# Two transformer blocks on one core: the first norm's sum of squares on VectorE, one statistics pass for two norms in a row, and the end of the delta rule reordered

## The reference, cut to what matters

```python
x = first_block(x, attn_norm, w_in, ..., final_norm)      # DEPTH = 2 layers, ends with a norm
return second_block(x, c_2, ctx_2, ...)                   # one layer, starts with a norm

def rmsnorm(x, g):                                        # first block, its last line included
    return x * rsqrt(mean(x * x) + EPS) * g
# second block
hl = modulate(rmsnorm_2(xl, g_pre_mix[i]), sh1l, sc1l)    # the "recurrent" norm
hc = modulate(rmsnorm_2(xc, g_pre_mix[i]), sh1c, sc1c)    # the same for 256 context positions
... = mixer_inputs(hl, w_in) ; mixer_inputs(hc, w_in)     # projections ab, qkv, u, z
ol = bidir_gdn(ql, kl, vl, bl, gl, s_f, s_b)              # gated delta rule, 64-position chunks, both ways
y_f = fourier_mix(u, w_f)
y_d = rmsnorm_2(o, g_gdn) * silu(z)
y = concat([y_f, y_d]) @ w_out
xl = xl + gt1l * rmsnorm_2(y, g_post_mix[i])
```

## Time and profile before

| | us |
|---|---|
| median of 3 runs | 3139.52 |
| the three runs | 3134.92 to 3141.40 |
| the profiled execution: its time | 3141.11 |
| the profiled execution: its span, first to last instruction | 3139.3 |

### The profile page before, as it was taken

One profiled execution on the slowest core, in us unless ns is written; L12 is line 12 of the kernel. 1 busy time (PEld: TensorE's weight loads), 2 busy tenths in 40 slices (PEclk: granted clock), 3 DMA queues, 4 the chain that ended last, 5 costly groups with the idle time before them and its releaser, 6 DMA issues.

```text
span 3139.3 us, 41302 instructions
## 1 busy us (share of the span) xinstructions
PE 2963.7 (94%) x16704; PEld 2338.8 (75%) x16704; DVE 1448.9 (46%) x2527; ACT 738.4 (24%) x1585; POOL 1625.7 (52%) x1134
## 2 busy tenths in 40 slices
PE   6999999999999999999999999999899987699998
PEld 5767777777777877677777777778778676578886
DVE  2654443354555027544433545552342377277721
ACT  3333332112111023333321111211122223211110
POOL 5434445556555663344455565556535254556664
PEclk9999999999999999999999999999899999899999
DMA  5433444545666544344444456665434000345554
GB/s 183 164 121 134 147 142 168 170 149 173 230 233 225 193 161 169 122 144 138 148 161 154 154 167 235 242 231 189 153 121 147 1 3 22 107 147 189 199 189 141
DMA packets 133565, 491.99 MB, mean 157 GB/s; under 512 B 14832, under 2 KB 14832, under 8 KB 132608
## 3 DMA queue, kind: packets, MB, share of 16 engines
q1 hardware_dynamic: 70736, 260.86, 25.4%
q0 software_dynamic: 61200, 222.85, 19.7%
q10 hardware_dynamic: 1440, 5.64, 0.5%
HBM read 487.17 MB, written 2.13 MB: 156 GB/s over the span
## 4 chain that ended last, share of the span: by engine, by line
PE 82%; DVE 7%; POOL 5%; issue 3%; DMA 2%; ACT 1%; POOLq 0%; DVEq 0%; ACTq 0%
PE dense L740 22%; PE dense L742 21%; PE dense L741 21%; POOL raw_lo L2476 2%; PE scores L944 2%; PE O L978 2%; PE turned L966 1%; POOL squares_sum L2494 1%; PE scores L740 1%; PE scores L741 1%; PE scores L742 1%; DMA weights_hi<-stream 1%; PE O L1012 1%; DVE row_sum L1959 1%; PE dense L1136 1%
## 5 line engine op out<-in xcount | busy, mean ns | idle before, releaser
L2476 POOL TENSOR_TENSOR raw_lo<-raw,weights_hi 128x1024 fp32r<-128x1024 f32 x425 | 1021.9, 2405 | 81.6 <-DMA raw<-stream 38.9
L740 PE MATMUL dense<-h_hi,weights_hi 128*128 128x512 f32 x2208 | 890.3, 403 | 14.8 <-DVE h_lo L1783 10.2
L742 PE MATMUL dense<-h_hi,raw_lo 128*128 128x512 f32 x2208 | 867.3, 393 | 0.0
L741 PE MATMUL dense<-h_lo,weights_hi 128*128 128x512 f32 x2208 | 867.0, 393 | 0.0
L2466 POOL DMA_DIRECT2D weights_hi<-stream x425 | 244.8, 576 | 1169.1 <-PE dense L742 1058.6
L740 PEld LDWEIGHTS dense<-h_hi,weights_hi 128*128 128x128 f32 x2208 | 418.8, 190 | 141.7 <-issue 55.4
L742 PEld LDWEIGHTS dense<-h_hi,raw_lo 128*128 128x128 f32 x2208 | 418.4, 189 | 90.8
L741 PEld LDWEIGHTS dense<-h_lo,weights_hi 128*128 128x128 f32 x2208 | 419.4, 190 | 80.8
L740 PE MATMUL dense<-hidden_hi,weights_hi 128*128 128x512 f32 x528 | 206.2, 390 | 0.0
L741 PE MATMUL dense<-hidden_lo,weights_hi 128*128 128x512 f32 x528 | 205.6, 389 | 0.0
L742 PE MATMUL dense<-hidden_hi,raw_lo 128*128 128x512 f32 x528 | 205.5, 389 | 0.0
(11 more groups left out here) (374 smaller groups left out, 4427.5 us busy)
## 6 DMA issues: line engine op xcount, KB each, us to landing
raw<-stream SPq DMA_DIRECT2D x473, 512.0 KB, 3.5
weights_hi<-stream POOLq DMA_DIRECT2D x425, 512.0 KB, 4.6
decays<-stream ACTq DMA_DIRECT2D x8, 512.0 KB, 4.5
gates<-f_scratch SPq DMA_DIRECT2D x2, 1536.0 KB, 9.6
x<-x_in SPq DMA_DIRECT2D x2, 1024.0 KB, 8.3
dft<-dft SPq DMA_DIRECT2D x4, 512.0 KB, 6.7
out<-x SPq DMA_DIRECT2D x4, 512.0 KB, 2.6
const<-consts ACTq DMA_DIRECT2D x1, 1024.0 KB, 10.8
```

Source lines behind the costliest of these rows:

```text
L740: nc.tensor.matmul(to, wh, xh, start=first, stop=False)
L741: nc.tensor.matmul(to, wh, xl, start=False, stop=False)
L742: return nc.tensor.matmul(to, wl, xh, start=False, stop=final)
L2476: nc.gpsimd.tensor_tensor(lo, src, hi, ALU.subtract).then_inc(weights_lo, 1)
```

## The change

It has three parts.

1. **Start.** `const` is loaded in two parts: first the 512 columns from `ident` on (256 KB), then `cos`, `sin` and `tri` with a semaphore of their own (`rope_landed`), for which DVE, POOL and PE wait at later places. ACT squares all eight chunks into eight slots of their own; DVE adds them in seven additions. `norm_stats((0,1))` has one source, so four matmuls in place of eight. PE no longer waits for `init_done` before it. POOL waits for the second half of `x` alone, issues three weight loads, subtracts item 0, and only then waits for `init_done` and makes the power; item 1 comes after it.
2. **Between the blocks.** Norm "f" is gone. During the `down` products of layer 1 ACT squares each chunk twice, as it is and scaled by `final_norm`, and POOL adds both. One `norm_stats("L")` has 16 matmuls, one power has 8 columns, `norm_rows` makes the rows of the product of both norms and then those of the final norm alone. `xT` itself is scaled later, in pairs of chunks during qkv 1 to 4 (`final_x`). PE's order is ab (context), statistics, half of qkv 0, rows, the rest of the context blocks. The loads of `dft` and `wf` move behind the raw load of qkv 2 and wait for the eight chunks of "L".
3. **End of the delta rule.** The Fourier half's high parts are made by ACT in group 0 and its low parts by POOL in group 1. In steps 8 to 11 POOL adds `oscan` into `o2` before DVE adds the `dense` part. `w_out`'s first three items are subtracted two after step 8 and one after step 9. The position blocks 1 and 2, complete after step 9, are squared, summed and scaled during steps 10 and 11; the power is taken in two halves of 8 columns; the blocks go in the order `T_ORDER`.

```diff
+T_ORDER = (1, 2, 0, 3)
 # SP
-                if item == (1, "down", FC - 2):
-                    sp.wait_ge(hidden_lo_ready, DEPTH * FC)
-                    sp.wait_ge(h_ready, 8 * (NORMS["X"] + 1))
+                if item == (TAIL, "qkv", 2):
+                    sp.wait_ge(h_ready, 8 * (NORMS["L"] + 1))
                     for i in range(4):
                         sp.dma_start(dft[i], dft_in[i]).then_inc(s_dft, 16)
                     sp.dma_start(wf, wf_in).then_inc(s_dft, 16)
 # PE
+                if name == (0, 1):
+                    pe.wait_ge(first_added, 1)
+                for last_one in range(1 if name == (0, 1) else 2):
...
+                if name == "L":
+                    pe.wait_ge(f_added, ACC_STEPS)
+                    pe.wait_ge(f_squared, KC)
+                    for src in (acc_f, square_f[:, 1, :]):
+                        for t in range(TB):
+                            last = nc.tensor.matmul(O[:, TB + t:TB + t + 1], src[:, t * P:(t + 1) * P], ones[:, 0:1], ...)
...
-            pe.wait_ge(s_init, INITS)
...
-            norm_stats("f")
-            norm_rows("f")
-            fill(len(EARLY) * KC)
+            fill(KC)
             norm_stats("L")
+            fill(KC // 2)
             norm_rows("L")
+            fill(KC + KC // 2)
             fill(3 * KC)
...
-            for t in range(TB):
-                pe.wait_ge(p_dve, P_MEANS + t + 1)
+            for n, t in enumerate(T_ORDER):
+                pe.wait_ge(p_scaled, n + 1)
+                pe.wait_ge(c_o1, 2 * latent_no(STEPS))
 # ACT
-            act.dma_start(const, const_in).then_inc(s_const, 16)
+            act.dma_start(const[:, at:CONST_N], const_in[:, at:CONST_N]).then_inc(s_const, 16)
+            act.dma_start(const[:, 0:at], const_in[:, 0:at]).then_inc(rope_landed, 16)
...
-            squares("f", x_chunk(DEPTH - 1, "down"), xT)
-            squares("L", lambda k: act.wait_ge(h_ready, 8 * NORMS["f"] + k + 1), xT)
+            squares("L", x_chunk(DEPTH - 1, "down"), xT)
...
+                    if g == 0 and lev < LEVELS - 1:
+                        act.wait_ge(qk_ready, 2)
+                        nc.scalar.activation(four_hi[:, lev - 1, :], yT[:, lev - 1, :], ACT.Copy).then_inc(four_rounded, 1)
...
             for s in range(STEPS - 4, STEPS):
                 output_state(s)
+                if s == STEPS - 2:
+                    output_squares(0, 2 * latent_no(s))
+            output_squares(2, 2 * latent_no(STEPS))
 # DVE
+            for k in range(1, KC):
+                dve.wait_ge(squared, k + 1)
+                ...
+                nc.vector.tensor_tensor(acc, first, first_squares[:, k, :], ALU.add).then_inc(done, 1)
...
-            norm_var("f")
-            for k in range(KC):
-                norm_scale("f", k, lambda k: sm("final_norm", k), xT, xT)
-            norm_var("L")
+            nc.vector.tensor_scalar(eps_var[:], O[:, TB:2 * TB], EPS / D_MODEL, EPS * EPS, ...)
+            nc.vector.tensor_scalar(n_var[:, TB:2 * TB], O[:, TB:2 * TB], 1.0 / D_MODEL, EPS, ...)
+            nc.vector.scalar_tensor_tensor(out=n_var[:, 0:TB], in0=O[:, 0:TB], scalar=1.0 / D_MODEL, in1=eps_var[:], ...)
             shifted("L", 0, 0, 0, hx, xT, SEQ, KC)
...
+                if c in (1, 2, 3, 4):
+                    final_x(2 * c - 2)
+                    final_x(2 * c - 1)
...
             for s in range(STEPS - 4, STEPS):
                 new_values(s)
+                if s == STEPS - 1:
+                    output_scale(0)
                 new_state(s)
+                if s == STEPS - 2:
+                    output_sums(0)
+            output_sums(2)
+            output_gate(0)
+            output_scale(2)
+            output_gate(2)
 # POOL
-            pool.wait_ge(s_init, INITS)
-            pool.wait_ge(s_const, 16)
-            for step in range(2):
-                issue(step)
-            for step in range(1, KC - 1):
-                add_square((0, 1), step)
+            pool.wait_ge(s_x[1], 16)
+            for step in range(3):
+                issue(step)
+            low(0)
+            pool.wait_ge(s_init, INITS)
             norm_pow((0, 1))
-            low(0)
             low(1)
-            issue(2)
...
-            norm_pow("f")
+            norm_pow("L")
             low(N_LAYER_WEIGHTS + 2)
-            for step in range(1, KC - 1):
-                add_square("L", step)
-            norm_pow("L")
...
+                    if g == 1 and lev < LEVELS - 1:
+                        four_low(lev - 1)
...
+            add_output(8, kd_ready, 2 * UNITS)
+            low(W_OUT)
+            low(W_OUT + 1)
+            add_output(9, weights_lo, W_OUT + 2)
+            low(W_OUT + 2)
+            add_output(10, weights_lo, W_OUT + 3)
+            output_pow(0)
+            add_output(11, p_pow, 1)
+            output_pow(1)
             issue(W_OUT + 3)
```

More of the change, by code:

```diff
@@ L880, in norm_rows @@
                 last.then_inc(rows_ready, 1)
+                if name == "L":
+                    for t in range(TB):
+                        last = nc.tensor.matmul(turned[:, 0, t * P:(t + 1) * P],
+                                                rstd[:, TB + t:TB + t + 1].broadcast_to((P, P)), ident,
+                                                start=True, stop=True)
+                    last.then_inc(both_var, 1)
             def open_misc(l, what):
@@ L1366, in square_of @@
                     act.wait_ge(square_added, number * ACC_STEPS + max(1, k - 2))
+                if name == "L":
+                    at = SMALL["final_norm"] + k
+                    nc.scalar.activation(square[k % 2], src[:, k, :], ACT.Square, scale=small[:, at:at + 1]).then_inc(squared, 1)
+                    if k >= 2:
+                        act.wait_ge(f_added, max(1, k - 2))
+                    nc.scalar.activation(square_f[:, k % 2, :], src[:, k, :], ACT.Square).then_inc(f_squared, 1)
+                    return
                 nc.scalar.activation(square[k % 2][:, 0:n], src[:, k, 0:n], ACT.Square).then_inc(squared, 1)
@@ L1557, in _ @@
                 if l == 0:
-                    squares((0, 1), lambda k: act.wait_ge(s_x[k // 4], 16), xT)
+                    for k in range(KC):
+                        act.wait_ge(s_x[k // 4], 16)
+                        nc.scalar.activation(first_squares[:, k, :], xT[:, k, :], ACT.Square).then_inc(squared, 1)
                 else:
@@ L2398, in _, with output_sums, output_scale @@
                 w_and_u(g)
+            def output_sums(first):
+                for n in (first, first + 1):
+                    dve.wait_ge(p_sq, n + 1)
+                    nc.vector.tensor_reduce(osum[:, n * GH:(n + 1) * GH], heads(SQ4[n]), AX_X, ALU.add).then_inc(p_sum, 1)
+                both = osum[:, first * GH:(first + 2) * GH]
+                dve.wait_ge(p_sum, first + 2)
+                nc.vector.tensor_scalar(both, both, 1.0 / GD, EPS, ALU.mult, ALU.add).then_inc(p_var, 1)
+            def output_scale(first):
+                dve.wait_ge(p_pow, first // 2 + 1)
+                for n in (first, first + 1):
+                    o = heads(o2[T_ORDER[n]])
+                    nc.vector.tensor_tensor(o, o, per_head(oscale[:, n * GH:(n + 1) * GH]), ALU.mult).then_inc(p_scaled, 1)
@@ L2399, in _, with output_gate @@
+            def output_gate(first):
+                for n in (first, first + 1):
+                    t = T_ORDER[n]
+                    dve.wait_ge(p_turned, n + 1)
+                    z = zT[:, :, t * P:(t + 1) * P]
+                    nc.vector.scalar_tensor_tensor(out=z, in0=heads((bankB + bankA)[n]), scalar=half_gdn[:, 0:1], in1=z,
+                                                   op0=ALU.mult, op1=ALU.mult).then_inc(p_gated, 1)
             for s in range(STEPS - 4, STEPS):
                 new_values(s)
+                if s == STEPS - 1:
+                    output_scale(0)
```

152 lines of the change are left out of this document (90 added, 62 removed).

## The result

The changed kernel takes 3117.0 us in the median of four runs (3115.4 to 3120.4), the kernel before beside it 3138.8 (3134.9 to 3141.4): ratio 0.9935, 95% interval 0.9923 to 0.9946. That is faster by 21.8 us. The forecast was 3114.0, a gain of 25.6, with the range 3105 to 3122. The profiled execution took 3116.6 with a span of 3114.8, 24.5 less than the profiled execution before.

The account below looks back on a forecast made before the run. PE is busy 94% of the span, so only its standstills can be won: start 7.5, between the blocks 11.5, delta rule's end 7.0, less 0.4, is 25.6. From 3141.1 that gives 3115.5, adjusted to the median 3114; range 3105 to 3122.

Parts of the forecast that it names:

- low(0) ahead of power is the bound: Start: item 0's subtraction, awaiting its weight load, holds the power, which ends at 20.6 instead of 28.1; gain 7.5 us.
- my two readings of the queues: Start: POOL's load lands at 18.3 if it waits for SP's loads, 16.5 if sharing evenly; 17.1 taken.
- stays as it is: Start: the 5.3 us from the power's end to the first dense matmul remain unchanged.
- the lower bound of 6.2: Start: smallest gain in the forecast's range, in us, if POOL's weight load lands at 18.3.
- Rival A: Start: POOL's descriptors wait for DVE's seven additions, load lands at 18.9, gain 5.7, time 3116; 3 in 10.
- POOL's six more additions lie in `down` products of 15 us each ... cost nothing: Between the blocks: POOL's added work is covered and costs nothing; 7.7 us if that cover were gone.
- A wait for weights in the `down` products: Sign in the profile after that would show the forecast wrong; no size given.
- The term for the Fourier constants: Between the blocks: the 2.5 MB of `dft` and `wf` delay POOL's weight loads; 0.5 us taken.
- Rival C: Delta rule, steps 8 to 11: POOL's additions enter the recurrence, 10.4 us lost, time 3124.5; 0.5 in 10.
- B: Between the blocks: transfers hold weight loads back, half speed lasts through ab and qkv 0; gain 5, 3121; 1.5 in 10.
- D: Long dense stretches after the delta rule: clock at 1.2 GHz for longer, kernel slower than before; 2 in 100.
- E: Parts don't do what they say, such as the start still waiting at 12 us; 3132 or more; 3 in 100.

Follow-up runs that it names:

- power_first: The changed kernel with POOL's first power ahead of item 0's subtraction instead of behind it: 3114.9 us, ratio 0.9919.
- norms_only: The kernel before with only the part between the blocks changed: 3130.6 us, ratio 0.9975.
- late_add: The changed kernel with POOL's two additions of the first chunk's squares moved behind the next weight item's load and subtraction: 3115.2 us, ratio 0.9927.
- raws_late: The changed kernel with SP's third and fourth weight load held until POOL's first weight load has landed: 3113.8 us, ratio 0.9916.
- dft_later: The changed kernel with the Fourier constants loaded one by one behind the raw loads of qkv 4 to 8: 3113.2 us, ratio 0.9916.
- combo_stall: The changed kernel with power before subtraction, SP's two loads held, Fourier constants later, context low parts earlier; stall in `down` left in: 3112.2 us, ratio 0.9919.
- late_ctx_early: The changed kernel with the first chunk's additions moved later and DVE's context low parts one chunk of `down` earlier: 3113.5 us, ratio 0.9918.
- late_spread: The changed kernel with the first chunk's additions moved later and two context blocks between the halves of the statistics: 3120.4 us, ratio 0.9937.

## Why the prediction was right, and where it was wrong

**Start: right, 7.2 for 7.5, with some luck.** `x` landed at 10.35 (10.0), the first weight load at 18.3 (17.1), the power ended at 21.8 (20.6), and the first dense matmul started at 26.2 (26). The step "low(0) ahead of power is the bound" is shown by power_first. The landing was 1.2 late because the load started 0.5 later and took 7.6 us, above the 7.0 I had put between my two readings of the queues. So the power came 6.3 us earlier, not 7.5. I had written that the stretch from the power's end to the first dense matmul "stays as it is"; it went from 5.3 to 4.4 us, because DVE's first low part no longer stood beside POOL's second subtraction. I hadn't foreseen that, and without it the start would have been worth 6.3, near the lower bound of 6.2. Rival A gave 18.9 for the landing, which is near, but by the wrong mechanism. POOL issued its three loads in 1.81 us, 0.60 each, while DVE added; elsewhere an issue takes 0.58:

```profile
11.03 3.08 DVE L2103 TENSOR_TENSOR squares_sum<-squares_sum,first_squares 128x512 f32<-128x512 f32 x4 [0.53 <-ACT first_squares L1595]
```

The Trainium skill ("SBUF — State Buffer", section "SBUF: two separate sides") has VectorE operations of certain kinds lock POOL out of writing descriptors. No such hold-up shows here in the issues, whose rows cover the issuing instruction only. What the first-packet delay followed in these runs was SP's queue.

**Between the blocks: the stage itself right, 12.0 for 11.5, and the price put on `down` wrong.** The load of qkv 2 was issued 27.7 us after the end of `down` where it was 40.1 before: 12.4 earlier, forecast 12.5. The wait for `raw_lo` was 4.0 of the 3 to 6 I named. The step that failed is "POOL's six more additions lie in `down` products of 15 us each ... cost nothing". The cover was real for five of the six. I had checked it by POOL's load in a whole product, and not at the first chunk, where POOL waits for ACT's squares and has the next subtraction behind that wait. Already in the kernel before PE went on only 0.05 us after that subtraction ended. The price was 3.7 us, half of the 7.7 that I gave for lost cover; norms_only and late_add show it. It is as large as the difference between the forecast's gain and the measured one (25.6 and 21.8). That match is partly chance: between the two profiled executions the difference is 24.5, with the same loss in it. "A wait for weights in the `down` products" did stand among the signs of a wrong forecast, but no rival had it, with a chance or a price.

The term for the Fourier constants was sized against the kernel before (7.46 after 7.02: 0.44 for my 0.5). What I missed is that they could have been kept out of the way altogether, which is worth 1.9 us of waiting. Of the half-speed level there were 3.4 us just behind the statistics and 3.4 behind the wait for qkv 2: 1.7 us of work lost at the first, against my 0.5.

**End: right, 6.9 with the moved Fourier parts for 6.6.** The wait was 5.9 for 5 to 6. Rival C (POOL in the recurrence) had as its sign new waits of more than 3 us in steps 8 to 11. The longest wait there is 4.1 us, where the kernel before has one of 5.6, so none is new, though POOL's additions are in the chain now. The decay of step 9 still took 3.6 us instead of 1.3 beside POOL's subtraction.

**Rivals B, D and E** fell: 3.4 us at half speed at either place, and the total of such stretches fell from 147 to 124 us. The time I gave for C was a little off: from its own terms (18.6 us from the other parts, 7.5 won, 10.4 lost) it is 3123.8, not 3124.5.

## What to carry to other kernels

Where work is added to an engine's list, don't compare it with the engine's mean load in the stage. Go to the instruction behind which it is queued, and see what that one waits for and how much slack the next consumer has. Here the kernel before already showed it: PE went on 0.05 us after the subtraction ended, so 1.95 us more in front of it became 3.7. A gain in one place moved TensorE's clock in another (10.2 us at 1.2 GHz in place of 3.4), so after each edit read the granted clock in the neighbouring stages as well as the waits. And a transfer that nobody needs soon goes behind the one that somebody waits for, even across queues.

## What the runs showed of the hardware

- The first packet of a weight load issued by POOL mostly moved 1.3 us after the issue where no packet of SP's queue moved in that time (1.34 at 2613.3 us of the changed kernel). With the usual 80 to 150 packets of SP's it mostly moved after 2.0 to 2.5 us (median 2.27). With 240 and more it moved after 2.9 to 4.0 (60 cases in all traces, median 3.3), among them 17 of 3.7 to 4.0, nearly all at the start and before qkv 2. Single cases lie outside, as 4.7 us with 199 packets at 72 us of the kernel before. The number of packets is partly a measure of the delay itself, since a full queue keeps moving them (410 in 3.8 us). After the first packet the two queues shared about evenly. The Trainium skill ("DMA: Bandwidth & Descriptors", section "Queues, rings and completion order") says that an engine takes turns between the queues that have work; the trace agrees after the first packet, and not before it. That the first one waits for what SP has queued is what raws_late (2.7 us for 4.0) and dft_later (2.4 for 4.0) bear out; by what mechanism, no run here shows.
- A DVE operation with both operands in SBUF that starts beside one of POOL ends only after it. DVE's context low part took 2255 ns against a median of 420:

```profile
L2239 DVE TENSOR_TENSOR hx_lo<-hx,ctx_hi x8: 411/420/2255, 2190.4 to 2237.4; 128x256 fp32r<-128x256 f32 x8
```

  It started at 2235.2 and ended with POOL's subtraction (2234.83 to 2237.21). DVE's first low part in power_first took 2.69 for 0.70. An operation with one tensor operand in SBUF and its result there was held as well: `hx<-hx,mod` took 2.56 us for 0.35 at 2144.61 of the changed kernel, beside POOL's subtraction (2144.60 to 2147.00). `x<-dense,x` (line 2136), which reads TensorE's result `dense` from PSUM, TensorE's output memory, took 0.69 beside POOL's operations as elsewhere. The Trainium skill ("SBUF — State Buffer", section "SBUF: two separate sides") calls this an exclusive lock of a shared pair of ports, held for a whole instruction; these rows agree.
- At the statistics of the changed kernel and its variants the clock was granted at 1.2 GHz for 3.4, 6.8, 10.2 or 13.7 us, with the same matmuls. With the stall in `down` and the wait of 0.7 to 1.1 us ahead of the statistics it was 3.4 (six traces), with the stall alone 6.8 (one), with neither 6.8 (two), with the wait alone 10.2 and 13.7 (one each). So nothing I changed in their surroundings sets it alone: not the stall 80 us before (combo_stall: 6.8 with it), not the wait of 1 us ahead of them (late_ctx_early: 6.8 without it, changed kernel: 3.4 with it), not blocks in between (late_spread: 13.7). This stays open.
